# Latent attention with three pairs of score banks and two banks of sums, projections in the idle sums bank; one range fold for both rotary tables, rotary products kept as own rows

## The reference

```python
mod = jax.nn.silu(c) @ ada_w[l] + ada_b[l]          # six vectors of D: sh1, sc1, ga1, ...
h = rmsnorm(x, g) * (1 + sc1) + sh1
q_lat, kv_lat, k_rope, ... = split(h @ w_in)
q = einsum('bsr,rhd->bshd', rmsnorm(q_lat, g_q), w_uq)
q_pe = apply_rope(q[..., 64:], pos)
kv = einsum('bsr,rhd->bshd', rmsnorm(kv_lat, g_kv), w_ukv)   # k_nope, v
k_pe = apply_rope(k_rope, pos)                       # one for all heads
s = (q_nope @ k_nope.T + q_pe @ k_pe.T) * 96 ** -0.5 # causal
y_mla = softmax(s) @ v
```

## Time and profile before

| what | value |
|---|---|
| three runs | 1393.14, 1397.28, 1434.07 us; median 1397.28 |
| the profiled execution | 1395.63 us |
| its slowest core's span | 1394.0 us (cores 1389.4 to 1394.0) |
| granted clock of PE, mean of that core | 0.987 |
| busy: PE, DVE, ACT, POOL | 1283.1, 632.3, 655.7, 201.4 us |
| first and last exponential of the latent attention | 149.9, 480.0 us |

### The profile page before, as it was taken

The page is one execution under the profiler, slowest core; times in us unless marked ns, Lnnn a source line. Parts: engine busy times, 40 slices in busy tenths (PEclk is TensorE's granted clock), DMA queues, the critical chain, the costliest instruction groups (busy, mean ns, idle before and its releaser), DMA issues.

```text
span 1394.0 us, 20354 instructions; the slowest of 8 cores (1389.4 to 1394.0 us)
## 1 busy us (share of the span) xinstructions
PE 1283.1 (92%) x7010; PEld 587.4 (42%) x7010; DVE 632.3 (45%) x860; ACT 655.7 (47%) x901; POOL 201.4 (14%) x174
## 2 busy tenths in 40 slices
PE   0778889999999899999999999999999999999996
PEld 0533444444444353232444444444444444444442
DVE  2578665666662114324222222664443443443356
ACT  0387778979889716849322222443003103202333
POOL 3000435220035101000233322010000000000000
PEclk9999899999999999999999999999999999999999
DMA  9982754130353205020442524386214204000014
GB/s 168 215 110 41 152 119 102 46 62 1 61 73 86 40 1 54 1 27 1 130 44 27 54 31 61 122 115 98 31 14 78 31 1 79 13 1 1 1 61 181
DMA packets 95250, 88.20 MB, mean 63 GB/s; under 512 B 36768, under 2 KB 79824, under 8 KB 95056
## 3 DMA queue, kind: packets, MB, share of 16 engines
q0 software_dynamic: 72640, 51.03, 27.3%
q1 hardware_dynamic: 22512, 35.89, 8.0%
...
## 4 chain that ended last, share of the span: by engine, by line
PE 81%; ACT 7%; issue 4%; DVE 3%; DMA 3%; SPq 1%; ACTq 0%; DVEq 0%; POOL 0%; another core or an unknown queue 0%; POOLq 0%
PE psb L452 81%; ACT arena L457 7%; DMA arena<-eoh 1%; SPq L275 1%; DVE arena L461 1%; DMA scr<-arena 1%; DVE arena L477 1%; DVE arena L473 1%; DMA arena<-xo 1%; DVE arena L469 0%; DVE arena L466 0%; ACTq L314 0%; DVEq L314 0%; ACT L457 0%; POOL arena L461 0%
## 5 line engine op out<-in xcount | busy, mean ns | idle before, releaser
L452 PE MATMUL psb<-arena 128*128 128x512 bf16 (+7 forms) x7010 | 1283.1, 343 | 99.9 <-ACT arena L457 34.4
L452 PEld LDWEIGHTS psb<-arena 128*128 128x128 bf16 (+4 forms) x7010 | 587.4, 100 | 795.3 <-issue 265.6
L457 ACT ACTIVATE arena<-psb 128x1024 bf16<-128x1024 f32 (+5 forms) x479 | 370.6, 822 | 124.5 <-PE psb L452 121.5
L457 ACT ACTIVATE arena<-psb,arena 128x512 f32<-128x512 f32 x220 | 150.7, 687 | 461.5 <-PE psb L452 396.1
L461 DVE TENSOR_TENSOR arena<-psb,arena 128x512 f32<-128x512 f32 (+4 forms) x228 | 148.0, 661 | 321.9 <-ACT arena L457 217.2
L461 DVE TENSOR_TENSOR arena<-arena 128x512 bf16<-128x512 f32 (+2 forms) x176 | 128.9, 732 | 143.7 <-ACT arena L457 136.3
L457 ACT ACTIVATE arena<-arena 128x512 f32<-128x512 f32 (+3 forms) x196 | 137.9, 716 | 104.6 <-DVE arena L473 69.6
L473 DVE SCALAR_TENSOR_TENSOR arena<-psb,arena 128x512 f32<-128x512 f32 x160 | 120.2, 751 | 138.7 <-PE psb L452 137.9
L477 DVE CAST arena<-psb 64x512 bf16<-64x512 f32 (+1 forms) x126 | 86.8, 689 | 119.4 <-PE psb L452 117.9
L461 POOL TENSOR_TENSOR arena<-arena 128x512 bf16<-128x512 f32 (+1 forms) x56 | 97.5, 1741 | 200.5 <-DVE arena L461 185.9
L473 DVE SCALAR_TENSOR_TENSOR arena<-arena 128x512 bf16<-128x512 f32 (+5 forms) x106 | 80.8, 769 | 4.4 <-ACT arena L457 1.8
...
## 6 DMA issues: line engine op xcount, KB each, us to landing
...
```

Of the source, the lines that this page charges most:

```text
L452: S.op("pe", lambda e: e.matmul(out, lhsT=lhsT, rhs=rhs, start=start, stop=stop), reads=R, writes=Wr, sig=sig, cost=cost_of("pe", out, lhsT))
L457: S.op("act", lambda e: e.activation(out=out, in_=in_, func=func, **kw), reads=R, writes=Wr, cost=cost_of("act", out))
```

## The change

**Attention.** Scores get three pairs of banks (2 to 7), the sums two (bank 0 for even heads, 1 for odd). The back of a unit follows three fronts later (`LA = 3`), with four `Pt`. A step or modulation piece writes the sums bank of the other head, `1 - e`, when the planner counts that head's scaling done and at least two more units of the present chunk remain. The steps are sorted by group (K, V of groups g and 4 + g, then Q of g), and a step need be done only before the chunk that reads it. A modulation piece goes into chunk 3 where the bank and DVE are counted idle. For odd chunks of pairs 0 to 2 DVE copies the even head's 64 rows to `yt`, which frees bank 0; in pair 3 every chunk takes the reciprocal.

**Rotary parts.** Query rows 64 to 95 now hold t cos, rows 96 to 127 the swapped halves by signed sin; the key rows hold the summed rotary key twice. The score matmul over 128 rows adds both products, so `qr_build` makes two products and no sums. In `x_group` one product-sum on 64 rows and one sum replace two and one, and three small SP copies a group spread the key rows. The weight block of the rotary columns is 64 wide instead of 96 (`KVC` 192), and `w_uq`'s columns are reordered.

**Tables.** One range fold serves both: ten DVE operations of 1024 after the cast instead of 22; scale and bias go into ACT's Sin.

**Loads and planner.** POOL issues pieces 2, 3, x group 0, pieces 0, 1, then x group 1 and on. `wukv` and `wuq` wait for piece 2's result instead of x group 0's load. The scheduler's assumed rates and costs change. In `x_group` DVE squares half of x for own groups too, and K, V, Q are built in banks 5 and 6.

```diff
-        bw = 0.0
+        bw = 5.0
-                    done = done + 2.0 + t["bytes"] / 50e3
+                    done = max(done, 4.0) + 2.0 + t["bytes"] / 15e3
-                    bw = max(bw, done) + t["bytes"] / 180e3
+                    bw = max(bw, done) + t["bytes"] / (150e3 if t["e"] == "pool" else 300e3)
...
-        for i in range(4):
+        def ada0_load(i):
             S.dma("pool", ada0[i], kc_src(adaw_d, 512 * i, 512 * i + 512), ("ada0", i), writes=[("ada0", i)])
+        for i in (2, 3):
+            ada0_load(i)
...
-        for i in range(NXB):
+        x_load(0)
+        for i in (0, 1):
+            ada0_load(i)
+        for i in range(1, NXB):
             x_load(i)
...
+        ts("dve", angt, posf, ropec[:, 0:1], None, ALU.mult, None, ["posf", "small"], ["angt"])
+        ts("dve", kf, angt, 1.0 / TWO_PI, None, ALU.mult, None, ["angt"], ["kf"])
+        cp("dve", posi, kf, ["kf"], ["kint", "posi"])
+        cp("dve", kf, posi, ["kint"], ["kf"])
+        stt(angt, kf, -CW1, angt, ALU.mult, ALU.add, ["kf", "angt"], ["angt"])
+        stt(angt, kf, -CW2, angt, ALU.mult, ALU.add, ["kf", "angt"], ["angt"])
+        ts("dve", kf, angt, 1.0 / TWO_PI, None, ALU.mult, None, ["angt"], ["kf"])
+        stt(posf, kf, 0.5, kf, ALU.is_gt, ALU.subtract, ["kf"], ["posf"])
+        stt(angt, posf, 0.5, posf, ALU.is_gt, ALU.subtract, ["posf"], ["angt"])
+        stt(kf, angt, 0.25, angt, ALU.is_gt, ALU.subtract, ["angt"], ["kf"])
...
-            tt("dve", rt1[HA, :], PS(pb)[HA, :], tabO[HA, cs], ALU.mult, [("ps", pb), ("tabO", 0)], ["rt1"])
-            tt("dve", rt2[HA, :], PS(pb)[HB, :], tabO[HB, cs], ALU.mult, [("ps", pb), ("tabO", 1)], ["rt2"])
-            for e in range(2):
+            for e, hs in ((0, HA), (1, HB)):
                 qt, qk = q_tile(j, e)
-                rs_ = slice(32 * e, 32 * e + 32)
-                tt("dve", qt[R2, cs], rt1[rs_, :], rt2[rs_, :], ALU.add, ["rt1", "rt2"], [qk + (g, 1)])
+                tt("dve", qt[HB, cs], PS(pb)[hs, :], tabO[hs, cs], ALU.mult, [("ps", pb), ("tabO", 0), ("tabO", 1)],
+                   [qk + (g, 1)])
...
-            if own:
-                act(sq[:, 4:8, :], xb[:, 4:8, :], AF.Square, [xk], [("sq1", i % 2, 1)])
-            else:
+            if True:
                 tt("dve", sq[:, 4:8, :], xb[:, 4:8, :], xb[:, 4:8, :], ALU.mult, [xk], [("sq1", i % 2, 1)])
...
+            stt(rt1[HA, :], K_["t12"][HA, :], bvk[HA, 3:4], tab[HA, cs], ALU.add, ALU.mult,
+                [("t12", s_), "bvk", (tk, 0), (tk, 1)], ["rt1"])
+            tt("dve", Kb[0][0][R2, ks], rt1[0:32, :], rt1[32:64, :], ALU.add, ["rt1"], [("Kpe0", 0, G)])
+            for (e, p0) in ((0, 96), (1, 64), (1, 96)):
+                S.dma("sp", Kb[0][e][p0:p0 + 32, ks], Kb[0][0][R2, ks], ("kdup", G), reads=[("Kpe0", 0, G)],
+                      writes=[("Kdup0", G)], group=True)
...
-            sb = 2 + 2 * (k % 2)
+            sb = 2 + 2 * (k % 3)
-            ab = u_acc[(h, c)]
+            ab = e
...
-                if c % 2 == 1:
+                if c % 2 == 1 and j < 3:
                     act(R[hy, :], PS(ab)[hs, :], AF.Ln, [("ps", ab)], [("rr", e)])
-                    if e == 1:
+                    if e == 0:
+                        cp("dve", yt[HA, :], PS(ab)[HA, :], [("ps", ab)], ["yt"])
+                    else:
...
         for j in range(1, 4):
-            for G in range(8):
-                steps.append(("K", j, 0.22, 1.2, lambda j=j, G=G: k_build(j, G, 7)))
-                steps.append(("K", j, 0.4, 0.7, lambda j=j, G=G: v_build(j, G, 7)))
             for g in range(4):
-                steps.append(("Q", j, 0.44, 1.2, lambda j=j, g=g: qn_build(j, g, 7)))
-                steps.append(("Q", j, 0.44, 2.6, lambda j=j, g=g: qr_build(j, g, 7)))
+                for G in (g, 4 + g):
+                    steps.append(((j, g), 0.22, 1.4, lambda pb, j=j, G=G: k_build(j, G, pb)))
+                    steps.append(((j, g), 0.25, 0.7, lambda pb, j=j, G=G: v_build(j, G, pb)))
+                steps.append(((j, g), 0.44, 1.4, lambda pb, j=j, g=g: qn_build(j, g, pb)))
+                steps.append(((j, g), 0.44, 1.4, lambda pb, j=j, g=g: qr_build(j, g, pb)))
...
-                if first and c == 3:
-                    ada_piece(4 + h)
-                    pe_t[0] += 0.8
...
+                if last:
+                    own_inv = c % 2 == 0 or h >= 6
+                    d = 4.1 if own_inv else (0.7 if e == 0 else 1.5)
+                    dve_t[0] = max(dve_t[0], pe_t[0] + (0.0 if own_inv or e == 0 else 2.0)) + d
+                    acc_t[e] = dve_t[0]
+                elif c == 3 and not ada_done[h] and max(dve_t[0], acc_t[1 - e]) <= pe_t[0]:
+                    ada_done[h] = True
+                    ada_piece(4 + h, 1 - e)
+                    pe_t[0] += 0.8
+                    dve_t[0] = max(dve_t[0], pe_t[0]) + 0.2
+                elif steps and h // 2 + 1 >= steps[0][0][0] and k + 2 < len(units):
+                    rest = [x for x in units[k - LA + 1:k - LA + 4] if x[:2] == (h, c)]
+                    if len(rest) >= 2 and max(dve_t[0], acc_t[1 - e]) <= pe_t[0] + 0.4:
+                        do_step(1 - e)
```

199 lines of the change are left out of this document (96 added, 103 removed).

## The result

The changed kernel takes 1381.16 us (median of 3 runs, 1378.19 to 1381.8) against 1397.28 before. The ratio is 0.9894, 95% interval [0.9846, 0.9942]: about 1% faster, where the forecast was 1342 us, 4%, in a range of 1320 to 1367. Run once more on another chip it was at 0.9924 [0.9905, 0.9944]. Some executions of most kernels, the one before too, have a lower granted clock on the cores of a die (down to 0.81 of full speed, at 1607.76 us), and the ratios leave these out, so a median can stand above what its ratio says.

The account below looks back on a forecast made before the run. The prediction took PE to bound the attention and DVE's work to pace the x groups. From 1395.6 us it took 18 for the x groups and 36 for the attention, giving 1342 us, range 1320 to 1367.

Parts of the forecast that it names:

- The x groups: Stretch before the attention: new load order and less DVE work end it at 132 instead of 149.8, 18 us saved.
- it only guards the scaling at 33: Range fold cut from 22 to 10 DVE operations: about 10 us of DVE, none counted as gain.
- what costs nothing: Fold, 24 small rotary-key copies, two full copies, later weight loads and narrower weights: no time counted for any.
- three pairs of groups from there at 17.4 us each: x groups from 70.75: DVE work of 15.3 us a pair at 0.88 busy, ending at 123, plus 9 of tail.
- 118 is the earliest end: x groups' load limit: last group lands at about 106, then a chain of about 12 us.
- my floor: Attention: PE work of 3 x 70.3 + 63.5 = 274 us, against 330.2 taken.
- about 5%: Attention: waiting for a reciprocal or late cast, taking the first three pairs from 70.3 to 74 us each.
- A: Rival: x groups keep their length, only the attention gains 36; 1360 us, chance 0.13.
- B: Rival: in the attention the third pair of banks buys little, 11 us saved; 1367 us, chance 0.13.
- C: Rival: all is hidden, both stages come near their limits, 118 and 280; 1314 us, chance 0.08.
- D: Rival: slower, attention steps find the sums bank busy and PE holds scores behind DVE; 1428 us, chance 0.04.
- E: Rival: denser PE gets a lower granted clock, 0.84, so the attention gains nothing; 1378 us, chance 0.02.

Follow-up runs that it names:

- e_silu: Changed kernel with the sinks' exponential moved out of the planned x groups to behind the front end; ratio 0.9873, first large exponential at 158.8 us.
- e_after2: The changed kernel unaltered, run again on another chip as partner for later runs; ratio 0.9924, first large exponential at 156.4 us.
- e_wtab: Changed kernel with the scratch tile wtab allocated over stages 0 to 1 instead of stage 0 alone; ratio 0.9859, first large exponential at 147.6 us.
- e_silu_wtab: Changed kernel with the edits of e_silu and e_wtab together; counted runs 1380.3 and 1380.9 us, no ratio, first large exponential at 144.6 us.
- e_order: Changed kernel with the front end's old planner costs, load order and small-matmul order, keeping new banks and DVE squares; ratio 0.9801, first exponential at 145.5 us.
- e_att_c0: Changed kernel with sums of chunks 0 and 3, not odd chunks, inverted by Ln and Exp in the first three pairs; ratio 0.9898, attention 306.1 us.
- e_front_late: Whole old front end under the new attention, but weight loads wait as in the change; counted runs 1375.8 and 1376.8 us, first exponential 149.4.

## Why the prediction was wrong

By its own sum the span should be 1394.0 - 18 - 36 = 1340.0; it is 1376.6. Of the 36.6 us missed, 26.3 lie ahead of the attention (158.3 against 132), 9.7 in it (303.7 against 294), 0.6 behind.

**The x groups: the step that failed.** "Only pieces 2 and 3 make the scale, and they now go first" is true, and e_silu shows group 0 at 35.25, even before my 40. In the changed kernel the scaling came at 45.82, not 33, because DVE's fold (34.70 to 45.2) was in front of it: "it only guards the scaling at 33" was backwards. And the early start hardly mattered: of the 11 us that e_silu brings group 0 forward, 2.9 reach the attention. I followed the loads and DVE's busy time, and never asked what the moved relative-bias matmul issues and who is behind that. The prediction doesn't name its DMA at all, not even under what costs nothing, though the kernel before shows DVE waiting 4.1 us for `scr`. That the change delayed this write by 27 us, past the time at which the block's second owner wants it, is 8.8 of the 26.3 (e_after2 to e_wtab). The early exponential is 3.0 (e_wtab to e_silu_wtab). The 1.9 between the changed kernel and e_after2 are the difference of the runs (the medians agree, 156.5 and 156.4).

The other 12.6 (144.6 against 132) are "three pairs of groups from there at 17.4 us each". The stretches of e_silu_wtab:

```profile
60.00:100.00 40.00, 38.45 (x170) 21.51 (x170) 20.66 (x32) 21.30 (x29) 2.62 (x3) 0.77 1.02 144
100.00:144.60 44.60, 38.60 (x185) 17.02 (x184) 38.80 (x57) 36.72 (x60) 3.35 (x4) 0.93 0.22 38
```

DVE's work is what I priced, 20.66 + 38.80 = 59.5 us against 4 x 15.3 = 61. It is 87% busy from 100 on. But from 60 to 100 it is busy 52%, not 88: PE, not DVE, is the full engine there (38.45 of 40 busy), with the bias blocks in it until 73.6 and a granted clock of 0.77, that is, part of the time at 1.2 GHz instead of 2.4. I had given the bias blocks no price at all. How the 12.6 divide stays open: no run took the blocks or the clock away alone. The blocks' place is hardly most of it, for e_order, with more things of before, has them ahead of the groups, at a granted clock of 1.00, and starts the attention at 145.5, by the medians 2.6 ahead of e_silu_wtab.

The loads show what I had wrong behind them. "Its slot free at about 50 instead of 67.29" came true, and brought nothing: the fifth x load leaves at 45.0 in e_silu_wtab and lands at 84.5, in the kernel before it leaves at 67.3 and lands at 85.0; up to there the DMA share is 1.1 in both, with the loads ahead of it still under way. And "118 is the earliest end" took 12 us from the last landing to the attention. In the changed kernel the last x group lands at 124.2, not at 106, and the attention starts 34 us later; in e_silu_wtab it lands at 106.0, just as forecast, and the attention starts 39 us later; in the kernel before, 36 (113.5 to 149.9). So 20 us and more of that time are work and waits on the groups, those that had landed already among them, which the 12 us left out. A part may again be shared memory: `wkvxf`, which the bias matmuls read, lies under the K block too (bytes 94208 to 108544), and in e_wtab and e_silu_wtab the first K product stands right behind the last bias block, at 75.17 and 72.36. No kernel gave `wkvxf` memory of its own, so this has no price.

**The attention: right in its mechanism, a term too small.** The pairs took 78.8, 76.8, 77.3 and 70.8 against 74 and 68. PE's work was right; its forms in 158.3 to 462:

```profile
L453 PE MATMUL psb<-arena 128*128 128x512 bf16 x966 | 239.0, 379 | 12.9 <-DVE arena L462 7.9 <-ACT arena L458 3.9
L453 PE MATMUL psb<-arena 128*128 128x128 bf16 x476 | 65.2, 221 | 1.3 <-ACT arena L458 1.1
L453 PE MATMUL psb<-arena 128*128 128x384 bf16 x128 | 32.7, 329 | 0.0
L453 PE MATMUL psb<-arena 128*128 128x256 bf16 x126 | 26.1, 275 | 0.0
L453 PE MATMUL psb<-arena 128*128 128x1 bf16 x256 | 7.5, 163 | 3.6 <-ACT arena L458 3.1
```

966 + 119 + 96 + 63 = 1244 widths at 0.214 are 266 us, and with 7.5 for the modulation 274: my floor to the microsecond, as it must be, since the widths are those of the program. The mis-sized term is the waiting, "about 5%" and 4 more: 20 us against 303.7 - 274 = 30. Sixteen of these are waits that the view names (the other 14 have no name in it):

```profile
PE psb L453 <- ACT arena L458: 8.1, 10, 1.1
PE psb L453 <- DVE arena L462: 7.9, 6, 1.7
```

The longest come where chunk 0 turns into chunk 1, four times, when the sums bank is still under the reciprocal and the scaling; e_att_c0, which takes most of them away, is 4.5 us shorter on cores 0 to 3:

```profile
167.65 2.54 PE L453 MATMUL psb<-arena 128*128 128x512 bf16 x15 [1.66 <-DVE arena L462]
```

ACT's wait for PE went from 45.6 in 88 places to

```profile
ACT arena L458 <- PE psb L453: 28.6, 62, 1.7
```

where I wanted under 20; its 3.41 us pauses are gone, as said.

**The rivals.** A, the early part keeps its length, came nearest in what it says (1360): the length did not stay, it grew. B falls: the third pair alone is 12 us, where B left 11 for everything. C and D did not happen: the longest wait for DVE is 1.7 us and there are six. E falls: the granted clock in the attention is 0.99 to 1.00 with all eight cores in it. Its number, 1378, is that of the profiled execution (1378.19), by luck: it let the early part gain 18 and the attention nothing, and it was the other way round. The Trainium skill (TensorE: Matmul & The Clock Gate, Seeing it yourself) would have had the clock at 13/16; no row of a profile here shows that. "What costs nothing" held for the 24 small copies and the narrower weights, as the stage after is 914.6; it did not hold for the weight loads, whose late start cost 1.9 us in e_front_late, nor for the fold, which stood ahead of the scaling.
